# State-space stage of a two-layer mLSTM / S5 step: the taps are sent for by ScalarE's queue instead of SyncE's

## The reference, cut to what matters

```python
def s5_mixer(x, lam_re, lam_im, log_dt, b_re, b_im, c_re, c_im, d_skip, w_glu, h0_re, h0_im):
    ...                                            # a, bb from lambda, dt and b
    bu_re = jnp.einsum('blgc,gpc->blgp', u, bb_re)
    bu_im = jnp.einsum('blgc,gpc->blgp', u, bb_im)
    ...                                            # h[t] = a * h[t-1] + bu[t], complex
    y = (jnp.einsum('gcp,blgp->blgc', c_re.astype(f32), h_re)
         - jnp.einsum('gcp,blgp->blgc', c_im.astype(f32), h_im)
         + d_skip.astype(f32).reshape(S5_GROUPS, S5_GROUP) * u)
    y = jax.nn.gelu(y.reshape(B, L, D_MODEL)).astype(x.dtype)
    ag = jnp.einsum('bld,de->ble', y, w_glu)
    a, g = jnp.split(ag, 2, axis=-1)
    return a * jax.nn.sigmoid(g), h_re[:, -1], h_im[:, -1]
```

## Time and profile before

| | us |
|---|---|
| runs: median of 3 (lowest, highest) | 1308.04 (1307.98, 1310.59) |
| profiled execution, its own time | 1306.63 |
| its span, first to last instruction | 1304.8 |
| TensorE busy | 1266.8 (97%) |
| VectorE busy | 852.1 (65%) |
| ScalarE busy | 507.2 (39%) |
| GpSimd busy | 345.1 (26%) |

### The profile page before, as it was taken

How to read it: one execution, slowest core, us unless ns; L and a number is a source line. 1 busy time by engine, 2 the same in 40 slices (tenths; PEclk the granted TensorE clock), 3 DMA queues, 4 the chain that set the end, 5 groups by cost and what they waited for, 6 DMA issues and landing times.

```text
span 1304.8 us, 24650 instructions
## 1 busy us (share of the span) xinstructions
PE 1266.8 (97%) x10085; PEld 1231.4 (94%) x10085; DVE 852.1 (65%) x1246; ACT 507.2 (39%) x767; POOL 345.1 (26%) x353
## 2 busy tenths in 40 slices
PE   6999999999999999999999989999999999999997
PEld 5999997789999999999999988999999999999997
DVE  5663336867788488573585598434886785785785
ACT  5311136532453353341342234223542542542553
POOL 0001005535200000799999672222000000000011
PEclk9999999999999999999999999999999999999999
DMA  6222333313322322242223997223223224213212
GB/s 171 59 73 81 87 97 78 90 46 94 104 89 72 110 81 82 65 105 81 81 83 97 186 159 177 86 86 109 63 96 101 77 82 113 80 66 114 80 65 74
DMA packets 214411, 121.98 MB, mean 93 GB/s; under 512 B 34816, under 2 KB 210616, under 8 KB 214336
## 3 DMA queue, kind: packets, MB, share of 16 engines
q1 hardware_dynamic: 213504, 120.74, 34.5%
q10 hardware_dynamic: 832, 0.21, 0.1%
HBM read 110.18 MB, written 10.75 MB: 93 GB/s over the span
## 4 chain that ended last, share of the span: by engine, by line
PE 83%; DVE 9%; issue 2%; ACT 2%; DMA 2%; POOL 1%; SPq 0%; DVEq 0%; ACTq 0%; POOLq 0%
PE ps L405 59%; PE ps L2121 19%; DVE wlo L389 1%; PE ps L1864 1%; DMA raw<-in_mlstm_w_in 1%; DVE x L1666 1%; PE ps L2004 0%; DMA Cst<-in_state_mlstm_C 0%; DVE Htok L1550 0%; DVE ps L1804 0%; DVE rot L1803 0%; DVE ps L1801 0%; DVE rot L1792 0%; ACT qkvo L1054 0%; PE ps L1944 0%
## 5 line engine op out<-in xcount | busy, mean ns | idle before, releaser
L405 PE MATMUL ps<-xg_hi,whi 128*128 128x288 f32 x1424 | 305.2, 295 | 1.1 <-DVE wlo L389 0.5
L405 PE MATMUL ps<-xg_hi,wlo 128*128 128x288 f32 x1424 | 304.9, 295 | 0.0
L405 PE MATMUL ps<-xg_lo,whi 128*128 128x288 f32 x1424 | 303.6, 295 | 0.0
L405 PEld LDWEIGHTS ps<-xg_hi,whi 128*128 128x128 f32 x1424 | 228.4, 188 | 2.7 <-issue 1.1
L405 PEld LDWEIGHTS ps<-xg_lo,whi 128*128 128x128 f32 x1424 | 228.1, 188 | 0.0
L405 PEld LDWEIGHTS ps<-xg_hi,wlo 128*128 128x128 f32 x1424 | 227.8, 188 | 0.0
L384 ACT ACTIVATE whi<-raw 128x1024 fp32r<-128x1024 f32 x83 | 87.7, 1058 | 270.1 <-PE ps L405 262.5
L389 DVE TENSOR_TENSOR wlo<-raw,whi 128x1024 fp32r<-128x1024 f32 x83 | 129.3, 1557 | 61.0 <-ACT whi L384 60.8
L405 PE MATMUL ps<-hid_hi,whi 128*128 128x288 f32 x640 | 138.6, 297 | 1.5 <-DVE hid_lo L1813 1.0
L405 PE MATMUL ps<-hid_hi,wlo 128*128 128x288 f32 x640 | 137.0, 296 | 0.0
L405 PE MATMUL ps<-hid_lo,whi 128*128 128x288 f32 x640 | 136.4, 294 | 0.0
(11 more groups left out here) (402 smaller groups left out, 2200.0 us busy)
## 6 DMA issues: line engine op xcount, KB each, us to landing
raw<-in_ffn_w_up SPq DMA_DIRECT2D x64, 512.0 KB, 4.0
raw<-in_ffn_w_down SPq DMA_DIRECT2D x24, 1024.0 KB, 4.9
raw<-in_mlstm_w_in SPq DMA_DIRECT2D x25, 512.0 KB, 3.8
raw<-in_ffn_w_down SPq DMA_DIRECT2D x16, 512.0 KB, 3.7
raw<-in_s_w_glu SPq DMA_DIRECT2D x16, 512.0 KB, 3.8
raw<-in_mlstm_w_out SPq DMA_DIRECT2D x8, 512.0 KB, 3.8
late<-d_taps SPq DMA_DIRECT2D x32, 128.0 KB, 6.3
d_u<-unat SPq DMA_DIRECT2D x64, 36.0 KB
```

The lines of the kernel that those rows point to most:

```text
L405: last = nc.tensor.matmul(ps[:, 2 * s + c, 0:HN], w[:, s, k, :], a[:, k, c * HN:(c + 1) * HN], start=(k == 0 and n == 0), stop=(k == KT - ...
```

## The change

The four `load_taps` leave SyncE's program and go into ScalarE's: the first ahead of the square root, behind two waits (that `d_taps` is written, and that the last matmul of the MLP before is done); the second behind the columns of tiles 0 and 1; the third behind the two splits; the fourth at the end of turn 1 of the loop, behind the GELU of tile 0. The transfers themselves are the same.

```diff
@@ SyncE
-            def load_taps(j):
-                for i in range(T):
-                    sp.dma_start(taps_pair[j][i * GC:(i + 1) * GC],
-                                 d_taps[2 * j * P:(2 * j + 2) * P, i * GC:i * GC + P].rearrange("(g c) m -> c g m", c=GC)).then_inc(mt_in[j], 16)
-
-            sp.wait_ge(slab_done, product_no(I_GLU) - 1)
-            load_taps(0)
-            load_taps(1)
             load_u(2)
             store_u(KT - 1)
-            load_taps(2)
             load_u(3)
...
             store_y(0, range(T))
-            load_taps(3)
             fetch_y(0)
@@ ScalarE
+            def load_taps(j):
+                for i in range(T):
+                    act.dma_start(taps_pair[j][i * GC:(i + 1) * GC],
+                                 d_taps[2 * j * P:(2 * j + 2) * P, i * GC:i * GC + P].rearrange("(g c) m -> c g m", c=GC)).then_inc(mt_in[j], 16)
+
+            act.wait_ge(taps_out, 16)
+            act.wait_ge(slab_done, product_no(I_GLU) - 1)
+            load_taps(0)
             act.wait_ge(r2_pe, 1)
...
             columns(0)
             columns(1)
+            load_taps(1)
             split_hi(act, I_GLU, 0)
             split_hi(act, I_GLU + 1, 0)
+            load_taps(2)
             for i in range(KT + 1):
...
+                if i == 1:
+                    load_taps(3)
                 if i == KT:
```

## The result

The changed kernel takes 1317.25 us (median of 4 runs, 1316.02 to 1318.28), the kernel before 1308.43 in the runs beside it: +8.8 us; the ratio, taken over all runs and not from the medians, is 1.0064 (95% interval 1.0047 to 1.0081). Its profiled execution took 1316.02 us with a span of 1314.2, against 1306.63 and 1304.8.

The account below looks back on a forecast made before the run. TensorE was taken to bound most of the kernel, but VectorE's `states` chain this stage. Queue delay 2.7 plus DMA sharing 3.9 made +6.6 us, moving the median from 1308.04 to 1314.6 us, range 1308.0 to 1319.7.

Parts of the forecast that it names:

- What bounds the stage, and that a late `gains_out` is not won back: VectorE's `states` run tile after tile, 6.39 us apart without gaps; a delay that makes one late stays to the end.
- The queue fills up and holds the engine that issues: After twelve taps issues the issuer waits for drains, 1.00 us each; without sharing, the 24th ends at 755.35, 32nd at 763.35.
- The first group, 0.45 us: Eight issues ahead of the square root take 3.9 us and delay it 0.45 us, no longer seen behind later delays.
- What sharing the DMA engines adds, half of 7.8, 3.9 us: SyncE's two stores and two loads beside the first 24 taps take 7.8 us alone; half is hidden, adding 3.9.
- Half clock at tile 3, taken as 0 and left in the upper end with 1.2: TensorE's `block_sums` of tile 3 at half clock costs between 0 and 1.2 us; 0 taken, 1.2 added to upper end.
- The sum: Tile 3's `states` late by 2.7 us from the queue with the taps alone, plus 3.9 from sharing: +6.6 us.
- the queue holds all the taps: Rival: ScalarE's queue takes all taps without stopping ScalarE; only 0.45 us is left, 1308.5 us; chance 16%.
- SyncE's relief: Rival: with fewer SyncE issues, stores and fetches go earlier at the stage's end, at most 1.0 us faster, 1307.0; chance 5%.
- the transfers add nothing: Rival: SyncE's transfers beside the taps cost nothing, leaving only +2.7 us, 1310.7; chance 10%.
- they add in full: Rival: SyncE's transfers cost the taps their full time, +10.5 us, 1318.5, up to 1319.7 with half clock; chance 19%.

Follow-up runs that it names:

- first group only: Changed kernel with only the first group of eight taps on ScalarE, the other three back in SyncE's program at their old places: 1310.33 us, ratio 1.0008.
- half the bytes: Changed kernel with 8 of 16 groups (64 KB) in every taps DMA, same 32 issues and places, part of y differs: 1308.39 us, ratio 0.999.
- spread: Changed kernel with the third and fourth groups issued four at a time at the ends of ScalarE's loop turns 1 to 4: 1309.15 us, ratio 0.9997.
- filler: Changed kernel with filler transposes on TensorE where it waits, for the square root and ahead of block_sums of tiles 2 and 3: 1317.75 us, ratio 1.0067.
- u later: Changed kernel with SyncE's loads of u and store of tile 7's u held until the third group of taps has landed: 1320.13 us, ratio 1.0086.
- alternate: Changed kernel with every group split, even steps on SyncE at its old places, odd steps on ScalarE: 1308.70 us, ratio 0.9998.
- behind the root: The version with later groups in fours, with the first group moved behind the square root and columns, fours ending turns 1 to 5: 1307.44 us, ratio 0.9995.
- last group on SyncE: Changed kernel with only the last group of eight taps back in SyncE's program behind the first store of y: 1312.99 us, ratio 1.0035.

## Why the prediction came out as it did

- *What bounds the stage, and that a late `gains_out` is not won back*: right. After tile 4 the beat is 6.4 us again and the stage ends 10.7 us late.
- *The queue fills up and holds the engine that issues*: right, and shown by halving the bytes, by spreading and by alternating. The 24th issue ended 21.9 us after the first (forecast 18.5 + 3.9 = 22.4).
- *The first group, 0.45 us*: too small. The eight issues took 4.65 us instead of 3.9, and the square root was 1.3 us late (740.24 against the sums' end at 738.96). TensorE then ran at half clock, which the forecast had not looked for there; tile 0 began 2.9 us late, counted from the first sums. None of it reaches the end, because tiles 2 and 3 are later still. Alone it was worth 2.5 us of the stage in "first group only" and "half the bytes" and 3.8 in "spread".
- *What sharing the DMA engines adds, half of 7.8, 3.9 us*: this is the term that was mis-sized. It was 6.4 up to the 32nd issue, or 5.4 by "filler". Two steps failed. The forecast put all this traffic beside the first 24 taps, where up to 3.2 us were added, and none beside the fourth group; but SyncE waited 11.4 us for `u`'s last store to land and sent for the last load of `u` at 755.05, and the last eight issues took 11.1 us instead of 8. And it took half as hidden, while over all 32 issues none was: the two loads and the store that "u later" held back are only 1.6 + 2.3 + 1.6 = 5.5 of the 7.8. Tile 6's store, the rest, cost next to nothing (18.7 against 18.5). That up to 6.4 were added where 5.5 were priced stays open.

  Both prices for sharing came from rows that don't hold what they were read for: 192 GB/s at 760 to 762 us had stores and taps of one queue at a change from one to the other, and in 126 GB/s, the price of a store, the first taps are in it (from 739.41). In the changed kernel, with tile 7's store beside the taps, 162 GB/s were moved at 744 to 750 us.

  The Trainium skill ("DMA: Bandwidth & Descriptors", section "Issuing engines are not separate DMA queues") says that DMAs run on the same 16 DMA engines whichever engine starts them. Taken strictly, as in the prediction, it was the better guide: the 5.5 us would be added in full, and 5.4 to 6.4 were.
- *Half clock at tile 3, taken as 0 and left in the upper end with 1.2*: it was 1.0 (2.19 against 1.22). "TensorE is at work again before that" was true, and not enough.
- *The sum*: 2.7 + 3.9 = 6.6 was forecast. With the measured sizes it is 2.7 + 6.4 + 1.0 = 10.1, and tile 3 began 771.94 - 735.54 = 36.4 us after the first issue against 762.98 - 736.85 = 26.1: +10.3. VectorE lost another 0.4 at tile 4, which makes the stage's 10.7. The profiled execution is 9.4 longer, not 10.7, because it reached the stage 1.3 us earlier, and the medians differ by 8.8.
- *The rivals*: that the queue holds all the taps is refuted by the trace. SyncE's relief gives nothing: with ScalarE's lateness removed (alternate, behind the root) the stage is 57.1 and 57.4, as before. That the transfers add nothing is refuted by "u later". That they add in full came nearest in the stage, +10.5 against 10.7, in part by luck: it counts 2.3 us for tile 6's store, which cost next to nothing, and leaves out the 1.0 of the half clock. The medians' 8.8 lie between it and the forecast.

## What to carry to other kernels

On ScalarE the first eight issues took 0.5 to 0.6 us each, with room in the queue, and ahead of the square root these were already enough to make it late. Once the queue was full an issue took up to 4.1 us. So compare the rate at which issues are made with the rate at which they drain (bytes by the GB/s of a stretch that holds only them), and where issues outrun the drain, look at what stands behind the last of them in program order. Idle time of an engine says nothing about it. Here four issues between two pieces of the loop's work, or half of them on each queue, cost nothing; sixteen ahead of a piece that another engine needs cost all that the queue took to drain.

## What the runs showed of the hardware that was not expected

- ScalarE's issues go ahead of arithmetic that stands before them, so "strictly in the order of its program" held only for its arithmetic, and for arithmetic behind an issue. The fourth group stands behind the first GELU in the program and began at 757.74, while `gains_out` still ran, which ended at 758.54; the GELU itself ran at 760.46. No wait stood between that was not met.
- The same eight first issues of ScalarE took 4.17 to 4.78 us in the seven profiles that have them at this place, 4.69 with half the bytes. SyncE's issues beside them don't explain it: in "last group on SyncE" it issued throughout and they took 4.21, in "u later" it had nothing to issue after 739.71 and they took 4.17.
- Beside the taps a store of eight DMAs of 36 KB landed late enough to hold SyncE's next load for 11.4 us; in "u later", with that store behind the taps, it was 3.9. SyncE's own wait in the changed kernel:

```profile
SPq L648 <- DMA d_u<-unat: 11.4, 1, 11.4
```

- After the wait for the late square root the granted clock was not the same in all versions. In "u later" and "last group on SyncE" TensorE had waited 1.27 and 1.30 us, and it went on at 2.4 GHz; in "first group only", the changed kernel, "half the bytes" and "spread" it had waited 1.42, 1.74, 1.78 and 1.87 us and was at 1.2 GHz for about 3 to 6 us. What decides it was not tested.
